# Partner swap for rope by a lane shuffle, router selection by match and replace, and the first attention's opening scores between two value blocks

## The reference, cut to what matters

```python
def apply_axial_rope(x, tab):               # rot_dim 64 in the first mixer, 32 in the second
    cos, sin = tab
    quarter = x.shape[-1] // 4
    xr, xc = jnp.split(x, 2, axis=-1)
    def rot(u, cs, sn):
        u1, u2 = jnp.split(u, 2, axis=-1)
        return jnp.concatenate([u1 * cs - u2 * sn, u2 * cs + u1 * sn], axis=-1)
    ...

def mixer_ab(...):                          # block 1, layer 0
    qa, ka = apply_axial_rope(qa, tab), apply_axial_rope(ka, tab)
    qb, kb = rope_diff(qb, tab), rope_diff(kb, tab)
    # window attention with sink (8 heads), differential attention (4 heads, two maps)
def mixer_mla(...):                         # block 1, layer 1
    qr = apply_axial_rope(qr, tab)
    kr = apply_axial_rope(kr, tab)

def moe_expert_choice(h, router_w, w_gate, w_up, w_down):   # block 2
    cap = CAPACITY_FACTOR * T // N_EXPERTS                  # 32 of 256 tokens
    aff = jax.nn.softmax(h @ router_w, axis=-1)
    gate, idx = lax.top_k(jnp.swapaxes(aff, 1, 2), cap)     # ties: the earlier token
    xs = h[bidx, idx]
    hid = jax.nn.silu(xs @ w_gate) * (xs @ w_up)            # 16 experts, 2048 wide
    ye = (hid @ w_down) * gate
```

## Time and profile before

| | us |
|---|---|
| median of 3 runs | 2424.35 |
| lowest and highest | 2421.68, 2424.43 |
| profiled execution, its time | 2422.87 |
| profiled execution, its span | 2420.9 |
| mean granted TensorE clock | 0.923 of full speed |

### The profile page before, as it was taken

The page is one execution under the profiler, slowest core; times in us unless marked ns, Lnnn a source line. Parts: engine busy times, 40 slices in busy tenths (PEclk is TensorE's granted clock), DMA queues, the critical chain, the costliest instruction groups (busy, mean ns, idle before and its releaser), DMA issues.

```text
span 2420.9 us, 28426 instructions
## 1 busy us (share of the span) xinstructions
PE 1986.5 (82%) x11571; PEld 1271.4 (53%) x11571; DVE 853.4 (35%) x1697; ACT 467.8 (19%) x1016; POOL 12.6 (1%) x23
## 2 busy tenths in 40 slices
PE   7989899999999999999999997755555565556555
PEld 4454488888548757999877885222111111111112
DVE  3156534555754555788265432100000000000001
ACT  3045542111002455211062222000000000000000
POOL 0000000000000000000000000000000000000000
PEclk9999999999999999999999998988877878877878
DMA  9202922221475621546933345999999999999997
GB/s 379 115 35 101 356 66 70 70 94 59 152 279 150 202 72 52 164 159 215 360 114 139 106 148 202 426 427 427 426 428 428 427 427 427 428 428 427 428 428 329
DMA packets 182177, 615.65 MB, mean 254 GB/s; under 512 B 26208, under 2 KB 122720, under 8 KB 148256
## 3 DMA queue, kind: packets, MB, share of 16 engines
q1 hardware_dynamic: 181264, 611.42, 64.9%
q0 software_dynamic: 784, 2.42, 0.3%
HBM read 612.77 MB, written 1.05 MB: 254 GB/s over the span
## 4 chain that ended last, share of the span: by engine, by line
PE 59%; DMA 36%; DVE 2%; ACT 2%; issue 1%; SPq 0%; POOL 0%; DVEq 0%; ACTq 0%
PE ps L401 58%; DMA ring<-in_expert_w_up 18%; DMA ring<-in_expert_w_down 17%; PE ps L885 1%; DMA ring<-in_ada_w 1%; ACT AR L940 0%; ACT AR L952 0%; PE ps L557 0%; DVE AR L827 0%; DVE X L828 0%; SPq L2709 0%; DVE H L822 0%; DVE ST L922 0%; DVE H L779 0%; ACT AR L1390 0%
## 5 line engine op out<-in xcount | busy, mean ns | idle before, releaser
L401 PE MATMUL ps<-ring,AR 128*32 128x256 f32 (+2 forms) x4336 | 556.9, 611 | 357.7 <-DMA ring<-in_expert_w_up 134.0
L401 PEld LDWEIGHTS ps<-ring,AR 128*32 128x32 f32 (+1 forms) x4336 | 191.2, 132 | 699.4 <-issue 229.3
L401 PE MATMUL ps<-H,ring 128*128 128x256 f32 (+3 forms) x2144 | 488.5, 384 | 2.7 <-ACT H L723 2.0
L401 PEld LDWEIGHTS ps<-H,ring 128*128 128x128 f32 (+1 forms) x2144 | 383.6, 191 | 89.3 <-issue 45.5
L401 PE MATMUL ps<-AR,ring 128*128 128x256 f32 (+2 forms) x1676 | 389.5, 388 | 3.9 <-DVE AR L1087 2.9
L401 PEld LDWEIGHTS ps<-AR,ring 128*128 128x128 f32 x1676 | 295.5, 190 | 88.3 <-issue 54.7
L2564 DVE TENSOR_TENSOR AR<-AR,ps 128x512 f32<-128x512 f32 x16 | 11.0, 687 | 580.8 <-PE ps L401 580.8
L401 PE MATMUL ps<-AR 128*128 128x128 f32 (+7 forms) x1200 | 166.1, 331 | 14.3 <-ACT AR L940 10.1
L401 PEld LDWEIGHTS ps<-AR 128*128 128x128 f32 (+4 forms) x1200 | 123.9, 179 | 44.0 <-issue 41.2
L2581 DVE TENSOR_TENSOR AR<-ps,X 32x256 f32<-32x256 f32 x60 | 25.2, 420 | 254.6 <-PE ps L401 253.1
L2550 ACT ACTIVATE AR<-ps 128x512 f32<-128x512 f32 x16 | 9.6, 597 | 522.2 <-PE ps L401 522.2
(11 more groups left out here) (324 smaller groups left out, 1504.8 us busy)
## 6 DMA issues: line engine op xcount, KB each, us to landing
ring<-in_expert_w_gate SPq DMA_DIRECT2D x64, 2048.0 KB, 28.2
ring<-in_expert_w_down SPq DMA_DIRECT2D x63, 2048.0 KB, 28.2
ring<-in_expert_w_up SPq DMA_DIRECT2D x61, 2048.0 KB, 28.2
ring<-in_ada_w SPq DMA_DIRECT2D x36, 2048.0 KB, 7.8
ring<-in_ffn_w SPq DMA_DIRECT2D x44, 1024.0 KB, 7.7
ring<-in_w_in SPq DMA_DIRECT2D x12, 2048.0 KB, 13.9
ring<-in_ffn_w SPq DMA_DIRECT2D x16, 1408.0 KB, 12.1
ring<-in_ab_w_in SPq DMA_DIRECT2D x4, 2048.0 KB, 19.9
```

The lines of the kernel that those rows point to most:

```text
L401: m = nc.tensor.matmul(out_, lhsT=lhsT, rhs=rhs, start=start, stop=stop)
```

## The change

**1. Rope.** `rotate` and both permutation tables go. VectorE puts each lane's partner, `lane ^ (dim // 4)` within 32 lanes, into the temporary by a `stream_shuffle`, and the sign that the permutation carried is now in the sine table. `dve_rope` has four instructions instead of three, and it waits for ScalarE's copy (the freed bank of the chunk) instead of for the rotation. This takes 8 rotations out of the projections, 6 out of the first attention, and 5 out of the second mixer. Their bank takes go too. The table's columns keep their place and size under new names.

**2. Router.** [...] After four rounds the selected tokens are those below zero. One running sum numbers them.

**3. Opening.** The scores of attention groups 0 to 2 (`pe_open`) stand between value blocks 1 and 2 of the projections. On ScalarE the exponentials of groups 0 and 1 (`act_open`) stand between its copies of those blocks. The second attention's opening is called right before its loop, as it was. VectorE's order there is unchanged.

```diff
@@ tables
-        perm = np.zeros((dim, dim), np.float32)
+        sin = np.sin(ang).astype(np.float32)
         for half in (0, 2 * q):
-            for i in range(q):
-                perm[half + q + i, half + i] = -1.0
-                perm[half + i, half + q + i] = 1.0
+            sin[half:half + q] *= -1.0
@@ Attention
+            def pe_open(self, pe):
+                for i in range(3):
+                    self.pe_scores(pe, i)
+
+            def act_open(self, c):
+                for i in range(2):
+                    self.act_exp(c, i)
@@ pe_ab_in
-                rotate(pe, cq - 2)
                 pe_dense(pe, ("qk", cq), w, (cq - 6) % 4 * P, H, T2)
             used()
-            rotate(pe, 12)
             w = ab_weights(pe, "bv")
             for t in range(4):
+                if t == 2:
+                    pe.wait_ge(roped.sem, roped_by(6, 10))
+                    attn0.pe_open(pe)
                 b = take(pe, ("vb", t))
...
-                if t == 0:
-                    rotate(pe, 13)
@@ dve_rope
+        def partners(dim):
+            return [lane ^ (dim // 4) for lane in range(32)]
+
+        def dve_rope(c, i, dst, key, tmp, cos, sin, dim):
+
+            freed(c.eng, key)
+            c.step(V.stream_shuffle(tmp, dst, partners(dim)))
+            c.step(V.tensor_tensor(tmp, tmp, sin, ALU.mult))
             c.step(V.tensor_tensor(dst, dst, cos, ALU.mult))
             c.mark(V.tensor_tensor(dst, dst, tmp, ALU.add), roped, i + 1)
@@ pe_mla_in
-            mm(ps[0:CQK, b, 0:TX], ft("perm_c", CQK, CQK), KR[0:CQK, 0:TX], True, True, b)
...
-                    if i < 2:
-                        rotate(2 * g + i)
@@ dve_mla_in
-                b = full_of(c.eng, ("rotm", i))
+                freed(c.eng, ("qr", i))
                 tmp = QT[:, i % 2, :]
-                c.free(V.tensor_tensor(tmp, ps[:, b, 0:TX], ft("sin_c"), ALU.mult), ("rotm", i))
+                c.step(V.stream_shuffle(tmp, QR[:, i, :], partners(ROPE)))
+                c.step(V.tensor_tensor(tmp, tmp, ft("sin_c"), ALU.mult))
@@ dve_route
-            for i in range(4):
+            for i, (src, dst) in enumerate(((aff, left), (left, over), (over, left), (left, over))):
                 c.step(V.max(TOP[0:NE, i, :], src))
-                if i < 3:
...
+                c.step(V.match_replace(dst, TOP[0:NE, i, :], src, -1.0))
+            c.step(V.tensor_scalar(even, over, 0.0, None, ALU.is_lt))
             c.step(V.tensor_tensor_scan(left, one, even, 0.0, ALU.mult, ALU.add))
-            c.step(V.scalar_tensor_tensor(out=even, in0=left, scalar=CNT[0:NE, 6:7], in1=even, op0=ALU.is_le,
-                                          op1=ALU.mult))
-            c.step(V.tensor_tensor(over, over, even, ALU.add))
-            c.step(V.tensor_tensor_scan(left, one, over, 0.0, ALU.mult, ALU.add))
-            c.mark(V.tensor_tensor(hit, left, over, ALU.mult), sel_ready, 1)
+            c.mark(V.tensor_tensor(hit, left, even, ALU.mult), sel_ready, 1)
```

More of the change, by code:

```diff
@@ L1407, in act_ab_in @@
             for t in range(4):
+                if t == 2:
+                    attn0.act_open(c)
                 b = full_of(c.eng, ("vb", t))
                 c.free(S.activation(VB[:, t, :], ps[:, b, :], ACT.Copy), ("vb", t))
-        def dve_rope(c, i, dst, key, tmp, cos, sin, rows=P):
-            b = full_of(c.eng, key)
-            n = int(np.prod(dst.shape[1:]))
-            rot = ps[0:rows, b, 0:n]
-            if len(dst.shape) == 3:
-                rot = rot.rearrange("p (a b) -> p a b", a=dst.shape[1])
-            c.free(V.tensor_tensor(tmp, rot, sin, ALU.mult), key)
+        def partners(dim):
[4 more added lines that the diff above has]
+            c.step(V.tensor_tensor(tmp, tmp, sin, ALU.mult))
             c.step(V.tensor_tensor(dst, dst, cos, ALU.mult))
@@ L2249, in build @@
         OUT = FLAT[:, 2 * D:4 * D].rearrange("p (t n) -> p t n", t=2)
-        LAST_SG, LAST_YE, LAST_GF = (FTAB[:, FT["perm_c"][0] + a * TX:FT["perm_c"][0] + (a + 1) * TX] for a in range(3))
+        LAST_SG, LAST_YE, LAST_GF = (FTAB[:, FT["room_c"][0] + a * TX:FT["room_c"][0] + (a + 1) * TX] for a in range(3))
         GFR, FWR = X[:, 0:4, TX:T2], X[:, 4:8, TX:T2]
@@ L2354, in dve_route @@
                 c.step(V.max(TOP[0:NE, i, :], src))
-                if i < 3:
-                    low = TOP[0:NE, i, 7:8]
-                    c.step(V.scalar_tensor_tensor(out=hit, in0=aff, scalar=low, in1=one, op0=ALU.is_ge, op1=ALU.mult,
-                                                  accum_out=CNT[0:NE, i + 1:i + 2]))
-                    c.step(V.scalar_tensor_tensor(out=left, in0=src, scalar=low, in1=src, op0=ALU.is_lt, op1=ALU.mult))
-                    src = left
-            at = PLACE[0:NE, :, :]
@@ L2362, in dve_route @@
-            c.step(V.tensor_tensor(at, ft("slot", 8, NE).unsqueeze(1).broadcast_to([NE, 4, 8]),
-                                   CNT[0:NE, 0:4].unsqueeze(2).broadcast_to([NE, 4, 8]), ALU.add))
-            c.step(V.scalar_tensor_tensor(out=at, in0=at, scalar=float(CAP), in1=TOP[0:NE, :, :], op0=ALU.is_gt,
-                                          op1=ALU.max))
-            least = CNT[0:NE, 4:5]
-            c.step(V.tensor_reduce(least, at.rearrange("p a b -> p (a b)"), axis=AX_X, op=ALU.min))
@@ L2369, in dve_route @@
-            c.step(V.scalar_tensor_tensor(out=over, in0=aff, scalar=least, in1=one, op0=ALU.is_gt, op1=ALU.mult,
-                                          accum_out=CNT[0:NE, 5:6]))
-            c.step(V.tensor_scalar(CNT[0:NE, 6:7], CNT[0:NE, 5:6], -1.0, float(CAP), ALU.mult, ALU.add))
-            c.step(V.tensor_scalar(even, aff, least, None, ALU.is_equal))
-            c.step(V.tensor_tensor_scan(left, one, even, 0.0, ALU.mult, ALU.add))
-            c.step(V.scalar_tensor_tensor(out=even, in0=left, scalar=CNT[0:NE, 6:7], in1=even, op0=ALU.is_le,
-                                          op1=ALU.mult))
```

52 lines of the change are left out of this document (16 added, 36 removed).

## The result

The changed kernel took 2392.95 us (median; 2390.6 to 2394.51), the kernel before 2424.39 beside it on the same chip (2421.68 to 2427.88). The ratio is 0.9866, 95% interval 0.985 to 0.9882: 31.4 us less. Between the two profiled executions it is 28.4 us (2422.87 and 2394.51), between their spans 28.3. The forecast was 21.6 us less, with a range of 2395 to 2409 us. The direction was right; the gain was larger than the range allowed.

The account below looks back on a forecast made before the run. The prediction took TensorE's path up to the expert stream, then the DMA engines, as the bound. Terms 3.8 + 4.0 + 1.6 + 6.5 + 2.1 + 3.6 = 21.6 us off 2422.87 gave 2401 us, range 2395 to 2409.

Parts of the forecast that it names:

- What bounds the kernel: Whole kernel: the expert stream starts when TensorE gets there, so a microsecond off before about 1508 us comes off the end.
- the standstill: DMA engines ahead of the experts: their idle time, with SyncE waiting 31.5 us for TensorE, would stay as long or longer.
- rests on the DMA engines: Rival at the experts: the expert stream does not follow TensorE, 2420 to 2423 us, no change; chance 0.04.
- a dear shuffle: Rival on VectorE, attention and projections: shuffles cost so much that the kernel slows, 2454 us at 6 us each; chance 0.03.
- Projections: Projections: eight rotations off TensorE give 3.4 us, with the first one's 0.35 us wait a term of 3.8 us.
- opening: First attention's start: TensorE's 4.03 us wait before the first transposes goes, the 1.06 stays; term 4.0 us.
- second mixer: Second mixer: five rotations off TensorE, which runs through there; term 2.1 us.
- the attention's term: First attention: six rotations removed, own time and waits together 6.5 us, ends 2.6 and 8.3.
- the 2.6 and two thirds of the 5.7: First attention: 2.6 us of rotations' own time, plus two thirds of 5.7 us in seven waits losing their cause.
- clock of 1.6: Opening of the first attention: without the idle time, full clock at 134 to 138 us; term 1.6 us, ends 0 and 1.7.
- The router's term: Router selection: 9.55 us becomes 5.9, a gain of 3.6 us, with 0.65 taken per match_replace; ends 2.7 and 4.7.
- more than the sum: Rival: all seven waits go, match_replace is a bare pass, clock rises earlier in the gathering; 2396 us, chance 0.08.

Follow-up runs that it names:

- the doubled shuffles: Changed kernel with each of its 19 shuffles issued twice, same operands; 2391.57 us, 0.2 below the changed kernel beside it.
- the takes kept: Changed kernel with each of the attention's six rotations replaced by a one-column product in a bank of its own; 2402.91 us, ratio 0.9919.
- the time kept: Changed kernel with 256-column products for five of the attention's six rotations put back, without bank takes; 2396.39 us, ratio 0.989.
- the shuffle alone: Changed kernel with the old router selection and old opening, so only rotations become shuffles; 2404.95 us, ratio 0.9919.
- the opening alone: Kernel before with only the opening scores and exponentials moved between the value blocks; rotations and old router stay; 2416.7 us, ratio 0.9973.

## Why the prediction was wrong in size

**What bounds the kernel** was right: the experts followed TensorE, at 427 GB/s. One of its signs was wrong, the standstill, which fell from 31.5 to 25.7 us and was to be as long or longer; the router and the gathering make it up, and they got shorter. No rival that rests on the DMA engines or on a dear shuffle had anything in it. A shuffle took 0.44 us and its lane list 0.01, as taken (0.45), and the doubled shuffles show the cover.

**Projections, opening, second mixer** came out as worked out: 4.0, 3.9 and 2.2 us against 3.8, 4.0 and 2.1. The second mixer, before and after, from the one product in front of it to the value copy of the earlier trace rows:

```profile
803.74 0.67 PE L401 MATMUL ps<-H,FTAB 128*128 128x256 f32 x2 [1.57 <-DVE H L779]
```

```profile
784.66 0.67 PE L397 MATMUL ps<-H,FTAB 128*128 128x256 f32 x2 [1.57 <-DVE H L775]
...
836.72 0.69 DVE L1750 COPY AR<-ps 128x512 f32<-128x512 f32 x1 [10.62 <-PE ps L397]
```

54.22 us before and 52.06 after.

**The step that failed is the attention's term**, "the 2.6 and two thirds of the 5.7", with its clock of 1.6: 8.1 us were forecast and 12.4 measured. The mechanism was right; three sizes in it were off.
- The waits. Seven of eleven were named as hanging on a rotation, 5.7 us, and then a third was struck off as coming back (two thirds of 5.7 are 3.8; 3.9 was entered). The waits on exponentials fell by 5.3 us and the idle time by 5.5. Not quite as named: of the seven, the 1.61 at 237.78 has a wait of 0.89 in its place (219.43 after), and of the four that were to stay, the longest shrank from 2.35 to 1.75. The experiment with the takes kept shows the cause as named (idle time +5.8). The reading of the order was right and the discount on it was a guess against the profile, in which both engines wait for TensorE there.
- The rotations' own time. 0.43 us is the price within a row of products, and the experiment with the time kept confirms it there (0.44). Here they cost 0.58 each, 3.5 us for six, since most stood alone behind a wait. The row was in view (first line: 0.70 us, part of it modelled end).
- The clock. 1.6 us were forecast for the opening. They came, but only as both edits were in. A second low stretch, at 219 to 224 us before, was missing in the changed kernel too, and nothing had been forecast for it. Its cause is open: the same wait of 1.75 us had a low stretch behind it in the kernel with the shuffle alone and in the one with the time kept, and a wait of 2.34 had none with the takes kept. The third stretch stayed, and was missing in one of the three profiles of the changed kernel.

**The router's term was mis-sized as well**: 3.6 forecast, 4.3 measured in the selection. The two instructions of a `match_replace` make 0.08 + 0.40 and not 0.65 us: the small one was priced like an instruction over 32 columns. What the prediction cited of the Trainium skill (Vector Engine (DVE) Microarchitecture Reference, 3.9), two instructions, is what the rows show; as one pass of 0.40 it would have been a forecast of 4.4 to 4.7, so the page was right, and the price put on its small instruction was too high. The comparison took 0.28 where 0.38 was taken. For the gathering nothing was taken; about 1 us belongs there on the mean.

**The rival "more than the sum"** (2396, chance 0.08) named three of these: all waits go, the cheaper match_replace, the earlier rise of the clock. It was the nearest of the cases, and still 3 us above the median. It did not have the rotations' own time (0.9 us more) nor the second low stretch (1.7), and its 2 to 3 us in the gathering were about 1. That its total came out near is in part luck.

**What stays open.** The medians differ by 31.4 to 32.7 us in the three comparisons, the profiled executions by 28.4. The changed kernel's profiled execution was the slowest of its four and lost 1.25 us ahead of the first changed place; before's was 1.5 us under its median. That explains the difference in kind, but no profile was taken of the other executions. What moves the first copy between 51.67 and 55.96 us, where the 1.3 us at the experts come from, and behind which waits the clock falls, was not tried.

## What to carry to other kernels

Count bank takes, not only instructions: a helper product that takes a bank out of turn costs its own time on TensorE and lengthens waits at the next scores; six of them cost 3.5 us by the first and 5.5 by the second. Where another engine idles, work such as a lane shuffle can be moved to it at no cost, as the doubled shuffles show here. If the profile says that the engines waited for are themselves waiting for TensorE, don't discount a wait whose cause goes.

Idle time ahead of dense products can cost twice, once as itself and once by the low clock behind it, here 1.7 us a time. Closing one gap is no promise that this second cost goes: in the kernel with the opening alone the low stretch stood behind the next waits. Filler products in a gap bought nothing here: the clock then fell behind them.

Before you give a difference of 1 or 2 us a cause, count the low stretches in both profiles and take them out of the busy time. Then the attention's own work agrees within 0.1 us between the three profiles of the changed kernel, whose times differ by 1.66.

## What the runs showed of the hardware

- LOAD_MASK_SELECT 0.01 us and STREAM_SHUFFLE 0.44 us for 128x256 float32, beside 0.42 for a tensor_tensor of that shape:

```profile
55.49 0.01 DVE L1408 LOAD_MASK_SELECT RS<-AR  x1 [6.43 <-ACT AR L1395]
55.52 0.44 DVE L1408 STREAM_SHUFFLE RS<-AR 128x256 f32<-128x256 f32 x1
```

- A pair of one-column products takes 0.35 to 0.38 us in the rows, about half of a pair with 256 columns (0.70) in the same place. By the attention's busy time with the low clock taken out, six such pairs cost 2.2 us, and six pairs with 256 columns 3.5.
- The same kernel loses 1.7 us to the low clock in the attention in two of three profiles and not in the other, with idle times of 10.57, 10.56 and 10.58 us. Its gathering took 5.45, 5.44 and 6.67 us. One profile cannot place a difference of that size.
